# One core, two transformer-like blocks: the S5 input projection in fp32 over paired modulation rows, four rows moved, joints and head steps reordered

## The chip, the cores and the metric

The kernel runs on one core of one Trainium2 chip. The metric is the device time of one execution in microseconds. 256 tokens go through two blocks of width 2048, and all weights come from HBM in fp32, some 700 MB.

## The reference, cut to what matters

```python
def rmsnorm(x, g):
    return x * rsqrt(mean(x * x) + eps) * g
c_act = silu(c)
sh_m, sc_m, gt_m, sh_f, sc_f, gt_f = split(c_act @ w_ada + b_ada, 6)
h = rmsnorm(x, g[0]) * (1 + sc_m) + sh_m
q, k, v, g_ret, u, gate_r, gate_s = split(h @ w_in)      # u is 1024 wide
ret = head_group_norm(retention(rope(q), rope(k), v))
y_ret = (silu(g_ret) * ret) @ w_ret_out
glu_a, glu_b = split(gelu(s5_ssm(u, ...)) @ w_s5_glu)
y = (sigmoid(gate_r) * y_ret + sigmoid(gate_s) * glu_a * sigmoid(glu_b)) @ w_out
x = x + gt_m * rmsnorm(y, g[1])
h = rmsnorm(x, g[2]) * (1 + sc_f) + sh_f
x = x + gt_f * rmsnorm(swiglu(h), g[3])
# second block: attention + gated linear attention + short conv, merged,
# then a swiglu, each added to x; the end is rmsnorm(x, final gain)
```

## The kernel before

**Layout.** Everything is held transposed: features on the 128 partitions, the 256 tokens along the free axis, so `x_res` is 128 x 16 x 256. A weight tile is 128 x 2048 fp32 (1 MB): 16 k-tiles of 128 x 128 for 128 output features. The weights run through a ring of four slots. For each tile SyncE issues the load (L498) once TensorE has let the slot go (`slot_free`), ScalarE makes a rounded copy `ring_hi` (`split_hi`, L859), VectorE makes the remainder `ring_lo` (`split_lo`, L1307), and TensorE multiplies it with the activations, which are split in the same way. A product of one k-tile is three matmuls of 256 columns in the stages with `thirds` (L520, L521, L522), else one of 512 and one of 256 (L523, L524). `ahead(p, g, m)` splits tile m+2 of stage p, body g, ahead of the work on tile m.

**Modulation.** `c_act @ w_ada` isn't done on TensorE. A modulation row (1 MB: 128 output features by 2048) lies in SBUF, and VectorE multiplies it with `c_act` and sums along the free axis (`ada`, L1329), then adds the bias (`modulation`, L1334). Rows 0 to 31 (shift and scale of the first block) make up the stage "ada", where they go through the four ring slots. All later rows are "asides": they travel in the same SyncE queue between weight tiles (L507) into one of two buffers of a stage, and wait for `aside_free`, the sign that VectorE has done with that buffer's last row. Rows 32 to 35 belong to the stage "u", and rows are spread over "heads", "glu", "out1" and "down1" too.

**Stages in order**: ada; u (8 tiles, the S5 input); heads (4 bodies of 12 tiles, two retention heads each); ret (32 tiles); glu (4 bodies of 8 tiles and 4 rows); out1; ffa, ffb, down1 (the first swiglu); att, gla, conv, mrg0, mix, out2 (the second mixer); ff2, down2. In glu an even tile gives a gate (16 k-tiles), an odd one the two halves of an output (8 k-tiles each), which VectorE merges with the gate (`glu_merge`, L1616 to L1618, and `merged_lo`, L1623).

**What sets the order.** Each engine's program is written out by hand, loop body by loop body, with counting semaphores in between; SyncE's queue is in order, so a load that waits holds all behind it. Four places matter here:

- *Opening.* `x` and small tables come in beside the first rows. ScalarE squares `x` (L885), TensorE sums the squares over the partitions (`add_squares`, L569), ScalarE takes the root (L889), VectorE the reciprocal (L1354). VectorE normalises (`norm`, L1362 and L1369) when all rows are done, ScalarE applies scale and shift (L905), and the u tiles are multiplied and brought out by ScalarE (`evac`, L872).
- *Heads.* Tile m has role r = m mod 6: q, k, v, v, g, g of a head. While a head's tiles are multiplied, the head before is finished: at r = 3 VectorE takes mean and variance of `p_o` (L1531 to L1535), ScalarE the root (`ret_step(3)`, L996), VectorE reciprocal and shift (`ret_before(4)`, L1538, L1539), ScalarE the scaled copy `o_t` (`ret_step(4)`, L1000), and TensorE turns it back (`ret_back`, L635) after the product of r = 5. Beside it runs the S5 chain (L1490 to L1497 on VectorE, L1984 to L1987 on GpSimd, L587 and L597 on TensorE).
- *Joints.* After out1, down1 and down2 stands a norm of the whole residual: sum of squares (`add_squares`, `add_features`), root, reciprocal, the residual sum in 16 steps (L1390, L1394), again squares and a root, and the new h.
- *Attention.* `att_scores`, `att_turn` (L723) and `att_values` follow the products of the three tiles of a head; VectorE normalises the softmax in between (`att_before`, L1738).

```python
def split_hi(p, g, m):
    act.wait_ge(raw_in[s], p.uses(g, m) * 16)
    run(hi[s][:, 0:n, :], raw[s][:, 0:n, :], COPY)
def ahead(p, g, m):
    split_lo(p, g, m + 2)
```

## Time and profile before

| | us |
|---|---|
| median of three runs | 3454.16 |
| their spread | 3452.05 to 3454.35 |
| profiled execution, its time | 3456.49 |
| its span in the trace | 3454.6 |
| TensorE busy in it | 3298.0 (95%) |
| VectorE busy | 2389.5 (69%) |
| ScalarE busy | 1494.9 (43%) |
| GpSimd busy | 445.8 (13%) |

The profile comes from one execution. PE is TensorE, PEld its weight load, DVE VectorE, ACT ScalarE, POOL GpSimd, SP SyncE and SPq its DMA queue. "clock" is the mean of the clock granted to TensorE, as a share of full speed: 0.982 over the whole execution. The name after "L" is a line of the program above. "idle before" says how long an engine stood still ahead of an instruction and which instruction ended that.

### The profile page before, as it was taken

To read this page: it belongs to the slowest core of one execution; us is meant where nothing else is said; L and a number is where in the kernel's file an instruction comes from. 1 tells how busy PE (TensorE), PEld (TensorE's weight loads), DVE (VectorE), ACT (ScalarE), POOL (GpSimd) and SP (SyncE) were. 2 spreads that over 40 slices of the span, in tenths; PEclk is the share of its full clock that TensorE was granted. 3 is DMA by queue.
4 is the path that set the end of the run, shared out by engine and by line. 5 is a ranking of instruction groups with operands and counts; after the bars stand their busy time and mean duration, and the time that the engine had idled before them with its cause. 6 is when DMAs were issued, how large, how long until landed. Compare 5 with 4: busy or idle time off the path is not lost.

```text
span 3454.6 us, 53480 instructions
## 1 busy us (share of the span) xinstructions
PE 3298.0 (95%) x20912; PEld 2990.6 (87%) x20912; DVE 2389.5 (69%) x2467; ACT 1494.9 (43%) x1538; POOL 445.8 (13%) x309
## 2 busy tenths in 40 slices
PE   1799999999989999999989999999999999999998
PEld 0799999999978888888868888888888888888887
DVE  8799987787676666655676667657767766666554
ACT  1455555544444344433354344344344444434332
POOL 2065556720100000000000000000002100000000
PEclk7899999999999999999999999999999999999999
DMA  9665554568745555567734444555555555555554
GB/s 399 269 235 219 217 206 173 187 246 302 300 151 184 194 186 190 190 233 258 266 111 167 171 159 175 191 182 190 193 183 198 185 190 187 193 185 190 190 190 146
DMA packets 111026, 706.34 MB, mean 204 GB/s; under 512 B 13376, under 2 KB 24256, under 8 KB 30672
## 3 DMA queue, kind: packets, MB, share of 16 engines
q1 hardware_dynamic: 100416, 693.86, 54.8%
q10 hardware_dynamic: 10512, 11.11, 1.0%
q8 instruction: 69, 1.13, 0.1%
q14 instruction: 29, 0.24, 0.0%
HBM read 702.83 MB, written 2.10 MB: 204 GB/s over the span
## 4 chain that ended last, share of the span: by engine, by line
PE 82%; DVE 8%; issue 4%; ACT 3%; POOL 2%; DMA 2%; DVEq 0%; ACTq 0%; POOLq 0%; SPq 0%
PE acc L523 44%; PE acc L524 23%; PE acc L520 4%; PE acc L521 4%; PE acc L522 4%; DVE ring_lo L1307 2%; ACT ring_hi L859 1%; DMA ring_raw<-w_ada 1%; DVE ring_raw L1329 1%; POOL s_w L1985 1%; PE p_norm L569 1%; POOL s_x L1987 0%; DVE aside_y L1329 0%; PE p_y L587 0%; POOL s_x L1984 0%
## 5 line engine op out<-in xcount | busy, mean ns | idle before, releaser
L1307 DVE TENSOR_TENSOR ring_lo<-ring_raw,ring_hi 128x2048 fp32r<-128x2048 f32 (+1 forms) x576 | 1312.4, 2280 | 571.8 <-ACT ring_hi L859 570.3
L523 PE MATMUL acc<-h_split,ring_hi 128*128 128x512 f32 x4736 | 1655.5, 392 | 9.2 <-DVE h_split L1369 4.5
L524 PE MATMUL acc<-h_split,ring_lo 128*128 128x256 f32 x4736 | 1337.5, 282 | 0.0
L859 ACT ACTIVATE ring_hi<-ring_raw 128x2048 fp32r<-128x2048 f32 (+1 forms) x576 | 1070.8, 1862 | 414.4 <-DMA ring_raw<-w_down 152.0
L523 PEld LDWEIGHTS acc<-h_split,ring_hi 128*128 128x128 f32 x4736 | 891.7, 188 | 197.3 <-issue 9.7
L524 PEld LDWEIGHTS acc<-h_split,ring_lo 128*128 128x128 f32 x4736 | 897.7, 190 | 0.4
L523 PE MATMUL acc<-ffn_split,ring_hi 128*128 128x512 f32 x1408 | 488.2, 390 | 0.0
L520 PE MATMUL acc<-h_split,ring_hi 128*128 128x256 f32 x1408 | 403.7, 287 | 82.9 <-DVE h_split L1369 69.8
L1926 POOL TENSOR_TENSOR sq_sum<-sq_sum,tile 128x256 f32<-128x256 f32 x60 | 76.6, 1277 | 2568.9 <-ACT tile L885 2568.9
L524 PE MATMUL acc<-ffn_split,ring_lo 128*128 128x256 f32 x1408 | 397.1, 282 | 0.0
L521 PE MATMUL acc<-h_split,ring_hi 128*128 128x256 f32 x1408 | 396.3, 281 | 0.0
L522 PE MATMUL acc<-h_split,ring_lo 128*128 128x256 f32 x1408 | 395.8, 281 | 0.0
L520 PEld LDWEIGHTS acc<-h_split,ring_hi 128*128 128x128 f32 x1408 | 267.9, 190 | 86.9 <-issue 82.9
L523 PEld LDWEIGHTS acc<-ffn_split,ring_hi 128*128 128x128 f32 x1408 | 264.4, 188 | 55.4
L521 PEld LDWEIGHTS acc<-h_split,ring_hi 128*128 128x128 f32 x1408 | 268.0, 190 | 0.8
L522 PEld LDWEIGHTS acc<-h_split,ring_lo 128*128 128x128 f32 x1408 | 267.9, 190 | 0.0
L524 PEld LDWEIGHTS acc<-ffn_split,ring_lo 128*128 128x128 f32 x1408 | 266.1, 189 | 0.0
L1140 ACT ACTIVATE ffn_split<-ffn_a 128x256 f32 (+1 forms) x88 | 36.8, 419 | 363.8 <-DVE ffn_a L1683 363.8
L1322 DVE TENSOR_REDUCE ffn_b<-acc 128x256 f32<-128x512 f32 x88 | 60.9, 692 | 146.3 <-PE acc L524 146.3
L885 ACT ACTIVATE tile<-x_res 128x256 f32 (+1 forms) x80 | 33.1, 417 | 150.3 <-DVE x_res L1907 83.9
L1138 ACT ACTIVATE ffn_t<-ffn_a 128x256 f32<-128x256 f32 x88 | 36.8, 418 | 130.3 <-DVE ffn_a L1679 119.1
L523 PE MATMUL acc<-mixed_split,ring_hi 128*128 128x512 f32 x256 | 89.9, 393 | 0.0
(342 smaller groups left out, 3814.2 us busy)
## 6 DMA issues: line engine op xcount, KB each, us to landing
ring_raw<-w_ff SPq DMA_DIRECT2D x88, 1024.0 KB, 4.8
ring_raw<-w_down SPq DMA_DIRECT2D x64, 1024.0 KB, 4.8
ring_raw<-w_ffb SPq DMA_DIRECT2D x56, 1024.0 KB, 4.8
ring_raw<-w_heads SPq DMA_DIRECT2D x48, 1024.0 KB, 4.8
ring_raw<-w_mix SPq DMA_DIRECT2D x48, 1024.0 KB, 4.8
ring_raw<-w_ada SPq DMA_DIRECT2D x32, 1024.0 KB, 7.4
ring_raw<-w_ret SPq DMA_DIRECT2D x32, 1024.0 KB, 4.8
ring_raw<-w_glu SPq DMA_DIRECT2D x32, 1024.0 KB, 4.9
```

The costliest lines, as they stand in the source:

```text
L520: mm(dst[:, 0:T], hi[s][:, t, :], moving[:, k, 0:T], start=start, stop=False)
L521: mm(dst[:, 0:T], hi[s][:, t, :], moving[:, k, T:], start=False, stop=False)
L522: return mm(dst[:, 0:T], lo[s][:, t, :], moving[:, k, 0:T], start=False, stop=stop)
L523: mm(dst[:], hi[s][:, t, :], moving[:, k, :], start=start, stop=False, skip_group_check=True)
L524: return mm(dst[:, T:], lo[s][:, t, :], moving[:, k, 0:T], start=False, stop=stop, skip_group_check=True)
L569: mm(p_norm[:, 0:T], ones[:], tile[kt % 2][:], start=kt == 0, stop=kt == KT - 1).then_inc(sq_used, 1)
L859: run(hi[s][:, 0:n, :], raw[s][:, 0:n, :], COPY).then_inc(hi_done, 1)
L1138: run(t[i % 2][:], a[i % 2][:], ACT.Tanh, scale=0.5).then_inc(f_tanh, 1)
L1140: run(dst[:, 4 * g + (first + i), 0:T], a[i % 2][:], COPY, scale=0.5).then_inc(f_hi, 1)
L1307: tt(lo[s][:, 0:n, :], raw[s][:, 0:n, :], hi[s][:, 0:n, :], SUB).then_inc(lo_done, 1)
L1322: v.tensor_reduce(dst, acc[o % 2][:].rearrange("p (c t) -> p t c", c=2), AX_X, ADD).then_inc(sum_done, 1)
L1926: tt(sq_sum[:], sq_sum[:], tile[b][:], ALU.add).then_inc(sq_used, 1)
```

## The change

It does five things.

1. **ada and u become one stage.** The 32 rows load in pairs, shift and scale of the same features, k and k+16, into four row buffers (`aside_y`, `aside_v`, `aside_u`, `aside_c`). The eight u tiles have places of their own (`u_weights`, and the raw buffers of ring slots 2 and 3) and load between the pairs, and so do the first two tiles of heads. VectorE has 16 steps of two rows and one `mod`, and takes the norm products between them. ScalarE applies scale and shift in place and makes h. TensorE multiplies in fp32 (no hi and lo): for each k-tile eight matmuls of 128 x 256 into eight banks. The lo part of h is made on GpSimd, in 16 subtractions.
2. **Rows 32 to 35 move from u to glu**, one to a body, as a fifth row (block number 12) in `aside_u`; VectorE takes it at the end of a body. SyncE's order in glu is a list, `GLU_ORDER`. The gain of out1 (`gain[:, 1]`) is made after glu.
3. **Joints.** The residual sums run over groups of feature tiles; in out1 the gain is applied when ScalarE brings the outputs out, in the last norm it is applied by ScalarE, and VectorE multiplies by the broadcast `rstd` in groups. Squares go through four buffers instead of two.
4. **Heads.** ScalarE brings v out ahead of the root of the head before; VectorE takes mean and variance after the S5 chain's part, and reciprocal and shift behind the `split_lo` of that tile. In ret the last head's steps stand one tile earlier.
5. **Attention.** Turn one tile later, values with the next head's first tile.

```diff
+        U_LOADS = {0: (0, 1), **{k: (k + 1,) for k in range(1, HALF - 1)}}
+        HEAD_LOADS = [5, 7]
+        GLU_ORDER = [(0, b) for b in (0, 1, 3, 4, 6, 7, 9, 2, 10, 5)] + [
+            (1, 0), (0, 8), (1, 1), (0, 11), (1, 3), (0, 12), (1, 4), (1, 2), (1, 6), (1, 7), (1, 5), (1, 9), (1, 10), (1, 8), (1, 11)]
+        for later in (2, 3):
+            GLU_ORDER += [(later, 0), (later, 1), (later - 1, 12)] + [(later, b) for b in range(2, 12)]
+        GLU_ORDER += [(3, 12)]
+
+        SUM_GROUPS = [(0, 2), (2, 2), (4, 4), (8, 4), (12, 2), (14, 1), (15, 1)]
+        OUT_GROUPS = [(0, 1), (1, 1), (2, 2), (4, 4), (8, 4), (12, 2), (14, 2)]
...
+            ada, p = dram["w_ada"].rearrange("g (j p c) -> (g j) p c", j=4, p=P), ph["u"]
+            for k in range(KT):
+                for r in range(2):
+                    n, use = (2 * k + r) % 4, (2 * k + r) // 4
+                    if use:
+                        sp.wait_ge(row_free[n], use)
+                    elif n == 3:
+                        sp.wait_ge(c_made, 1)
+                    sp.dma_start(row[n][:], ada[k + KT * r]).then_inc(row_in[n], 16)
+                for o in U_LOADS.get(k, ()):
+                    src = dram["w_u"][o // 4, p.offsets[o % 4]:p.offsets[o % 4] + KT * P * P].rearrange("(p c) -> p c", p=P)
+                    sp.dma_start(u_w[o][:].rearrange("p k c -> p (k c)"), src).then_inc(u_in, 16)
+                if k in HEAD_LOADS:
+                    m = HEAD_LOADS.index(k)
+                    at = ph["heads"].offsets[m]
+                    sp.dma_start(raw[m][:].rearrange("p k c -> p (k c)"), dram["w_heads"][0, at:at + KT * P * P].rearrange(
...
                         m, i = p.weights_until(at), p.asides_until(at)
-                        src = dram["w_" + name][g, offset:offset + n * P * P].rearrange("(p c) -> p c", p=P)
+                        if at < len(p.blocks):
+                            (kind, n), offset = p.blocks[at], p.offsets[at]
+                            src = dram["w_" + name][g, offset:offset + n * P * P].rearrange("(p c) -> p c", p=P)
+                        else:
+                            (kind, n), offset = ph["u"].blocks[4 + g % 2], ph["u"].offsets[4 + g % 2]
+                            src = dram["w_u"][g // 2, offset:offset + n * P * P].rearrange("(p c) -> p c", p=P)
...
+                            if name == "heads" and opening(g) and m < SLOTS:
+                                sp.wait_ge(u_summed, 2 * m - 2)
...
+            pe.wait_ge(std_done, 1)
+            pe.wait_ge(u_in, 16 * HALF)
+            for k in range(KT):
+                pe.wait_ge(now_done, k + 1)
+                for o in range(HALF):
+                    ins = mm(u_bank[o][:, 0:T], u_w[o][:, k, :], normed[:, k, T:], start=k == 0, stop=k == KT - 1)
+                    if k == KT - 1:
+                        ins.then_inc(u_summed, 1)
+                if k < KT - 1:
+                    ins.then_inc(u_used, 1)
...
+            def first_h():
+
+                act.wait_ge(n_done, KT)
+                for k in range(KT):
+                    act.wait_ge(mod_done, k + 1)
+                    run(normed[:, k, T:], normed[:, k, T:], ACT.Identity, bias=mod[:, k:k + 1],
+                        scale=mod[:, KT + k:KT + k + 1]).then_inc(now_done, 1)
+                    act.wait_ge(now_done, k + 1)
+                    run(h[:, k, 0:T], normed[:, k, T:], COPY).then_inc(n_hi, 1)
+                    if k - 2 in HEAD_LOADS:
+                        split_hi(ph["heads"], 0, HEAD_LOADS.index(k - 2))
+                    if k == 6:
+                        waves(0, 0)
+                    elif k == 8:
+                        cosines(0, 0)
+                for o in range(HALF):
+                    act.wait_ge(u_summed, o + 1)
+                    run(u[:, o, :], u_bank[o][:, 0:T], COPY).then_inc(u_done, 1)
...
-                        if r in (3, 4):
+                        if r == 4:
                             ret_step(r, g, i, n)
                     evac(p, g, m, m, (qk[:, 0, :], qk[:, 1, :], v_t[:, 0, :], v_t[:, 1, :], g_t[:, 0, :], g_t[:, 1, :])[r])
-                    if r == 0 and not (opening(g) and i == 0):
+                    if r in (0, 3) and not (opening(g) and i == 0):
                         ret_step(r, g, i, n)
                     if r == 3:
                         if not (opening(g) and i == 0):
...
-                                square_of(stage, acc[o % 2][:, 0:T], d, o % 2)
-                                evac(p, g, o, m, y[:, d, :])
+                                square_of(stage, acc[o % 2][:, 0:T], d, o)
+                                run(y[:, d, :], acc[o % 2][:, 0:T], ACT.Identity, scale=gain[:, 1, one(d)]).then_inc(evac_done, 1)
...
+                                if updates == 3:
+                                    run(x[:, d, :], x[:, d, :], ACT.Identity, scale=gains[:, 6, one(d)]).then_inc(x_scaled, 1)
...
+            act.wait_ge(gain_done, 1)
             down(ph["out1"], 1, y1, 1)
...
+                for j, (k0, n) in enumerate(SUM_GROUPS):
+                    for k in range(k0, k0 + n):
+                        ins = stt(y[:, k, :], y[:, k, :], gain[:, i, k:k + 1], rstd[:], MUL, MUL)
+                    ins.then_inc(y_times, 1)
+                    dve.wait_ge(y_times, len(SUM_GROUPS) + j + 1)
+                    at = slice(k0, k0 + n)
+                    tt(x[:, at, :], x[:, at, :], y[:, at, :], ADD).then_inc(y_done, n)
...
+            for k in range(KT):
+                at = 2 * (k % 3)
+                if k >= 3:
+                    dve.wait_ge(mod_done, k - 2)
+                for r in range(2):
+                    n, use = (2 * k + r) % 4, (2 * k + r) // 4
+                    ada(row[n][:], row_in[n], row_free[n], use + 1, at + r)
+                for r in range(2):
+                    dve.wait_ge(row_free[(2 * k + r) % 4], (2 * k + r) // 4 + 1)
+                both = slice(k, k + KT + 1, KT)
+                stt(mod[:, both], ada_sum[:, at:at + 2], 0.5, b_ada[:, both], MUL, ADD).then_inc(mod_done, 1)
...
+                if 3 <= k < 7:
+                    for t in range(4 * k - 12, 4 * k - 8):
+                        stt(normed[:, t, T:], x[:, t, :], gains[:, 0, t:t + 1], rstd[:], MUL, MUL).then_inc(n_done, 1)
+                if k - 3 in HEAD_LOADS:
+                    split_lo(ph["heads"], 0, HEAD_LOADS.index(k - 3))
...
-                    if prev[i] and r == 4:
-                        ret_before(r, g, i, n)
                     ahead(p, g, m)
-                    if prev[i] and r != 4:
+                    if prev[i] and r != 3:
                         ret_before(r, g, i, n)
                     s5_turned_back("heads", g, m)
+                    if prev[i] and r == 3:
+                        ret_before(r, g, i, n)
...
+                i = p.asides
+                ada(aside["glu"][0][:], aside_in[0], aside_free[0], p.aside_count(g, i), i)
+                dve.wait_ge(aside_free[0], p.aside_count(g, i))
+                own.step(stt(mod[:, one(g + 2 * KT)], ada_sum[:, i:i + 1], 0.5, b_ada[:, one(g + 2 * KT)], MUL, ADD))
                 own.leave(1 if opening(g) else p.iters - 1)
+            tt(gain[:, 1, :], mod[:, 2 * KT:3 * KT], gains[:, 1, :], MUL).then_inc(gain_done, 1)
...
-            residual(y1, 1, 2)
+            inverse_std(2)
+            dve.wait_ge(evac_done, ph["out1"].out_count(ph["out1"].iters - 1, 3))
+            for j, (k, n) in enumerate(SUM_GROUPS):
+                at = slice(k, k + n)
+                tt(y1[:, at, :], y1[:, at, :], rstd[:].unsqueeze(1).to_broadcast([P, n, T]), MUL).then_inc(y_times, 1)
+                dve.wait_ge(y_times, j + 1)
+                tt(x[:, at, :], x[:, at, :], y1[:, at, :], ADD).then_inc(y_done, n)
...
-                if r == 1:
+                if r == 2:
...
-            for kt in range(KT):
-                stt(x[:, kt, :], x[:, kt, :], gains[:, 6, kt:kt + 1], rstd[:], MUL, MUL).then_inc(out_ready, 1)
+            for k, n in OUT_GROUPS:
+                dve.wait_ge(x_scaled, k + n)
+                tt(x[:, k:k + n, :], x[:, k:k + n, :], rstd[:].unsqueeze(1).to_broadcast([P, n, T]), MUL).then_inc(out_ready, 1)
...
+            for k in range(KT):
+                pool.wait_ge(n_hi, k + 1)
+                if k < KT - 1:
+                    pool.wait_ge(u_used, k + 1)
+                else:
+                    pool.wait_ge(u_summed, HALF)
+                tt(h[:, k, T:], normed[:, k, T:], h[:, k, 0:T], ALU.subtract).then_inc(h_done, 1)
```

SyncE in glu, at the seam of two bodies (here bodies 1 and 2; 2 and 3 read alike). `slot_free` counts ring slots, `aside_free0` is that of `aside_u`. Before:

```order
L507 DMA aside_u<-w_glu 128x2048 [waits aside_free0,s5_done]
L507 DMA aside_s<-w_glu 128x2048 [waits aside_free1,s5_done]
L446 UNCONDITIONAL_BRANCH
L446 ISA
L498 ISA [waits slot_free0]
L498 DMA ring_raw0<-w_glu 128x2048
L498 ISA [waits slot_free1]
L498 DMA ring_raw1<-w_glu 128x2048
L506 REGISTER_ALU [waits s5_done]
L507 ISA [waits aside_free0]
L507 DMA aside_u<-w_glu 128x2048
L498 ISA [waits slot_free2]
```

With the change:

```order
L555 DMA aside_s<-w_glu 128x2048 [waits aside_free1,s5_done]
L544 DMA ring_raw0<-w_glu 128x2048 [waits slot_free0]
L544 DMA ring_raw1<-w_glu 128x2048 [waits slot_free1]
L555 DMA aside_u<-w_u 128x2048 [waits aside_free0,s5_done]
L555 DMA aside_u<-w_glu 128x2048 [waits aside_free0,s5_done]
L544 DMA ring_raw2<-w_glu 128x2048 [waits slot_free2]
L544 DMA ring_raw3<-w_glu 128x2048 [waits slot_free3]
```

Two rows for the same buffer now stand one behind the other, with the tiles for slots 2 and 3 behind them. At the way out of glu the fifth row of body 3 stands ahead of `x_res` and of the first tiles of out1:

```order
L544 DMA ring_raw3<-w_glu 128x2048 [waits slot_free3]
L555 DMA aside_s<-w_glu 128x2048 [waits aside_free1,s5_done]
L555 DMA aside_u<-w_u 128x2048 [waits aside_free0,s5_done]
L519 DMA x_res<-x_t 128x4096 [waits s5_done]
L459 UNCONDITIONAL_BRANCH
L459 ISA
L544 ISA [waits slot_free0]
L544 DMA ring_raw0<-w_out1 128x2048
```

In order before, `x_res` followed the `aside_s` row at once.

VectorE in heads at r = 3 and 4 (`gn_` are the retention norm's values, `s5_` the S5 chain's). Before:

```order
L1307 TENSOR_TENSOR ring_lo1<-ring_raw1,ring_hi1 128x2048 [waits hi_done]
L1531 BN_STATS gn_stats<-p_o 128x6 [waits ret_summed]
L1532 BN_STATS gn_stats<-p_o 128x6
L180 REGISTER_ALU
L1533 MEMSET gn_shift 128x2 [waits dve_own]
L1534 BN_AGGR gn_mean<-gn_stats 128x2
L1535 BN_AGGR gn_mean<-gn_stats 128x2
L1483 REGISTER_ALU
L1490 TENSOR_TENSOR s5_w<-p_z,s5_tab0 128x512 [waits s5_sine,scan_done,s5_cos,z_done]
```

With the change the S5 part comes first, and behind the statistics stands the next tile's lo, then the reciprocal:

```order
L1577 SCALAR_TENSOR_TENSOR s5_w<-s5_r,s5_w 128x256
L1611 BN_STATS gn_stats<-p_o 128x6 [waits ret_summed]
L1612 BN_STATS gn_stats<-p_o 128x6
L181 REGISTER_ALU
L1613 MEMSET gn_shift 128x2 [waits dve_own]
L1614 BN_AGGR gn_mean<-gn_stats 128x2
L1615 BN_AGGR gn_mean<-gn_stats 128x2
L1392 REGISTER_ALU
L1393 TENSOR_TENSOR ring_lo2<-ring_raw2,ring_hi2 128x2048 [waits hi_done]
L1618 RECIPROCAL gn_mean<-gn_mean 128x2 [waits ret_std]
L181 REGISTER_ALU
L1619 SCALAR_TENSOR_TENSOR gn_shift<-gn_mean 128x2 [waits dve_own]
```

So the scale of a finished head now waits for `ring_lo2`, which waits for ScalarE's `ring_hi2`.

## Rows read from the trace of the kernel before

**Rows 1.** The page: busy time by engine
```profile
PE 3298.0 (95%) x20912; PEld 2990.6 (87%) x20912; DVE 2389.5 (69%) x2467; ACT 1494.9 (43%) x1538; POOL 445.8 (13%) x309
```

**Rows 2.** Timeline of the opening: start, us, engine, line, operation [idle before]
```profile
37.49 0.16 DVE L1334 SCALAR_TENSOR_TENSOR mod<-ada_sum,b_ada_sb 128x4 f32 x1 [0.25 <-DVE ada_sum L1329]
...
98.05 1.91 ACT L859 ACTIVATE ring_hi<-ring_raw 128x2048 fp32r<-128x2048 f32 x1 [59.01 <-DMA ring_raw<-w_u]
...
106.99 0.55 PE L520 MATMUL acc<-h_split,ring_hi 128*128 128x256 f32 x1 [69.81 <-DVE h_split L1369]
...
155.69 1.28 ACT L937 ACT_TABLE_LOAD   x1
```

**Rows 3.** Busy time by stretch: length, PE, PEld, DVE, ACT, POOL; clock; DMA share; GB/s
```profile
20.00:40.00 20.00, 11.00 (x32) 5.95 (x32) 18.52 (x36) 10.29 (x22) 14.02 (x12) 1.00 1.00 403
...
401.00:405.00 4.00, 4.00 (x20) 4.00 (x20) 1.93 (x2) 3.31 (x6) 0.00 (x0) 0.50 0.00 0
```

**Rows 4.** Timeline of TensorE: heads, second head of a body; end of glu
```profile
399.35 0.58 PE L520 MATMUL acc<-h_split,ring_hi 128*128 128x256 f32 x1 [3.24 <-ACT v_t L872]
...
892.95 0.39 PE L520 MATMUL acc<-merged_split,ring_hi 128*128 128x256 f32 x1 [1.23 <-DVE merged_split L1623]
```

**Rows 5.** Timelines of ScalarE and TensorE in heads, first head of a body
```profile
353.69 0.29 ACT L996 ACTIVATE gn_mean<-gn_mean,eps 128x2 f32<-128x2 f32 x1 [9.03 <-DVE gn_mean L1535]
...
356.28 1.90 ACT L859 ACTIVATE ring_hi<-ring_raw 128x2048 fp32r<-128x2048 f32 x1
...
361.64 0.60 PE L635 MATMUL p_norm<-ident,o_t 128*128 128x128 f32 x4
```

**Rows 6.** Groups by line in the joint after out1: busy, mean ns | idle before
```profile
L1390 DVE SCALAR_TENSOR_TENSOR y<-y,gain,rstd 128x256 f32 x16 | 6.7, 480 | 0.4 <-DVE rstd L1354 0.4
L1394 DVE TENSOR_TENSOR x_res<-x_res,y x16 | 5.7, 419 | 0.0
```

**Rows 7.** Timeline and groups of TensorE in attention
```profile
1803.64 0.33 PE L723 MATMUL p_z<-ident,ex 128*128 128x128 f32 x1 [3.33 <-DVE ex L1738]
...
L723 PE MATMUL p_z<-ident,ex 128*128 128x128 f32 x4 | 1.1, 285 | 2.2 <-DVE ex L1738 2.2
```

**Rows 8.** Timeline of TensorE: fp32 matmuls of 256 columns, two records each
```profile
184.87 1.02 PE L587 MATMUL p_y<-s_x,s_c_sb 128*128 128x256 f32 x4
185.74 1.03 PE L597 MATMUL p_z<-u,s_b_sb 128*128 128x256 f32 x4
```

**Rows 9.** Timelines of GpSimd and VectorE side by side, in heads
```profile
360.67 3.39 DVE L1329 CUSTOM_DVE_ANT_0 aside_r<-aside_r,c_act 128x2048 f32<-128x2048 f32 x1
...
361.99 2.67 POOL L1986 TENSOR_TENSOR s_x<-s_w,s_x 128x256 f32<-128x256 f32 x1
...
363.99 2.81 DVE L1307 TENSOR_TENSOR ring_lo<-ring_raw,ring_hi 128x2048 fp32r<-128x2048 f32 x1
```

**Rows 10.** Timeline of VectorE in glu: end of body 1, and in body 3
```profile
801.86 0.43 DVE L1623 SCALAR_TENSOR_TENSOR merged_split<-val_a,merged_split 128x256 f32 x1 [0.72 <-ACT merged_split L1075]
...
874.25 2.28 DVE L1329 CUSTOM_DVE_ANT_0 aside_u<-aside_u,c_act 128x2048 f32<-128x2048 f32 x1
```

**Rows 11.** Timeline of SyncE's queue at a seam of glu and at its end
```profile
792.57 5.77 SPq L498 DMA_DIRECT2D ring_raw<-w_glu  x2
...
866.20 0.34 SPq L481 DMA_DIRECT2D x_res<-x_t  x1
869.94 5.77 SPq L498 DMA_DIRECT2D ring_raw<-w_out  x2
```

**Rows 12.** The page: loads, KB each, us from issue to landing
```profile
ring_raw<-w_ff SPq DMA_DIRECT2D x88, 1024.0 KB, 4.8
```

**Rows 13.** Timeline of ScalarE in glu and at the start of out1
```profile
806.22 0.38 ACT L872 ACTIVATE val_a<-acc 128x256 f32<-128x256 f32 x1 [0.53 <-PE acc L522]
...
880.79 1.92 ACT L859 ACTIVATE ring_hi<-ring_raw 128x2048 fp32r<-128x2048 f32 x1 [5.15 <-DMA ring_raw<-w_out]
...
899.34 0.39 ACT L885 ACTIVATE tile<-acc 128x256 f32<-128x256 f32 x1 [1.38 <-PE acc L522]
```

More of the change, by code:

```diff
@@ L95, in asides_in @@
     def asides_in(self, k):
-        return len(range(k, self.asides, self.beside))
+        return len(range(k, self.rows, self.beside))
     def aside_count(self, g, i):
@@ L131, in schedule @@
     }
-    for name in ("u", "ffa", "att"):
+    for name in ("ffa", "att"):
         ph[name].opens = True
-        ph[name].opening_lo = 4 if name == "u" else 3
-    for name in ("u", "heads", "ret", "glu", "out1"):
+        ph[name].opening_lo = 3
+    for name in ("heads", "ret", "glu", "out1"):
         ph[name].thirds = True
+    ph["glu"].rows += 1
     block = weight = 0
@@ L1454, in _ @@
[L1454 to L1466 removed]
+            own.step(v.tensor_scalar(b_ada[:, KT:2 * KT], b_ada[:, KT:2 * KT], 1.0, None, ADD))
@@ L1625, in _ @@
             for g in bodies(dve, p, first=1):
-                own.enter(4 * 2 + 1 + opening(g), g, first=1)
+                own.enter(4 * 2 + 2 + opening(g), g, first=1)
                 if opening(g):
```

228 lines of the change are left out of this document (110 added, 118 removed).

## The prediction

> **What bounds the kernel now.** I began with the page. TensorE is busy 3298.0 us of a span of 3454.6 [rows 1]. So an edit counts where it moves TensorE's work or an idle time of TensorE; a VectorE step beside a running product is free. I then read the timelines of the changed stages for the places where TensorE stands still.
>
> In the opening it sums squares and then waits 69.81 us, until 106.99 [rows 2]. DMA fills that time: its share is 1.00, at 403 GB/s [rows 3]. The hi of the first u tile starts at 98.05, when the tile has landed; 36.4 MiB have come by then (c 1, tables 0.4, x 2, 32 rows, one tile) since about 1.8 us, so 2.64 us per MiB. The last u output comes out just ahead of 155.69 [rows 2]: heads begins at 155.2. In glu TensorE idles only at the end, 1.23 us [rows 4]: nothing is to be gained there, but much to lose. In heads it waits once per body, 3.24 us, for ScalarE's copy of v [rows 4], which stands behind a root that waits for VectorE as in [rows 5]. After that wait the granted clock is 0.50, the lower of its two levels, 1.2 of 2.4 GHz [rows 3]; the product behind it took 8.5 us, where others take 5.6. I charge that difference, 2.9 us, to every idle time of three us or more. In a joint VectorE's 32 steps are the path, TensorE idle [rows 6]; in attention it waits for the softmax [rows 7].
>
> **The change, part by part** (minus is a gain).
>
> *Opening.* Three clocks run side by side. **DMA**: the last row is now the 45.4th MiB (32 rows, 8 u tiles, 2 heads tiles, 3.4 else) and lands at 1.8 + 45.4 x 2.64 = 121.8. **TensorE**: two fp32 matmuls take 0.87 us [rows 8], so the 128 take 55.7. They can start when row 13 (the 25.4th MiB, 69.0) is multiplied and the last norm products are made, at 74.2, and would end at 74.2 + 55.7 + 2.9 = 132.8. **VectorE**: a pair costs two rows at 2.25 and 0.6 for `mod` (0.16, with 0.25 of waiting before it and as much behind) [rows 2], 5.1 in all. Pair 8 is done at 87.6, since its rows land no sooner; seven more pairs and two lo parts of 2.3 give 127.9. On top come GpSimd's subtractions, some twelve in that stretch. In heads a row took 3.39 us beside GpSimd, 1.1 more than the usual 2.29, and a lo part 2.81, 0.5 more than usual [rows 9]. At 0.8 each that is 9.6: the last `mod` at 137.5, 0.5 on ScalarE and 3.5 for the last eight matmuls, 141.5. Heads begins **13.7** earlier. Ends: -22.4 if GpSimd costs nothing and TensorE's own work binds, -6 if all sixteen cost 1.1. Heads tiles 2 and 3 load only after `u_summed` 2 and 4, but land some 7 us later and are needed 11 us later: free.
>
> The Trainium skill, SBUF — State Buffer, section "Who interferes with whom", says that a VectorE operation with two SBUF inputs and a GpSimd one that reads SBUF exclude each other, and the one that comes second is blocked for the other's whole length. By that rule each of the twelve would cost its full length, and the opening would give 10.1, the sum below 3483. The rows bear out that they exclude each other, but one of the two lost only 0.5 us.
>
> *Rows 32 to 35.* Their VectorE work, 4 x 2.3 us, lies beside products wherever it stands. What counts is SyncE's queue. In glu's bodies 2 and 3, row (g-1, 12) is followed by the first row of body g for the same buffer, which waits until VectorE has taken the former, at the end of body g-1: `merged_lo` at 801.86 [rows 10], then the row until 804.6. Behind it wait the tiles for slots 2 and 3, issued at 792.57 before [rows 11], now at 805.3. A tile lands 4.8 after its issue [rows 12], 2.6 more behind another MiB: 812.8. ScalarE makes that tile's hi ahead of bringing out the gate, and TensorE needs the gate's bank for the second half product, which began at about 806.3, where `val_a` comes out [rows 13]. Now it begins at 812.8 + 1.9 + 0.4 = 815.1: idle 8.8, clock 2.9, **+11.5** rounded, twice. In body 1 the row stands loosely among its tiles: free.
>
> At the way out, row (3, 12) waits for that buffer's last row, done at 876.5 [rows 10], and `x_res` and out1's tiles stand behind it; before, they went at 866.20 and 869.94 [rows 11], and the hi of the first began at 880.79 [rows 13]. Now x, a row and a tile (4 MiB) follow 876.5: the hi starts at 888.8, the gate's bank is 7.9 late, and the clock costs 2.9. Then out1's first row waits for row (3, 12), multiplied behind the end of glu: 892.9 [rows 4], plus 8 to 8.5, plus 2.3, is 903.6. Out1's tile 2 stands behind: it lands at 911.3 and its lo is ready at 915.5, 918.4 with the clock's loss. Its product began at 898.9, just as the one before came out [rows 13]. That is **+19.6** for the whole way out. Glu in all: **+42.6**, low end 28 (no clock loss), high end 50.
>
> *Heads.* In the second head of a body the wait for v goes, -3.24 - 2.9, and `ret_back` then waits 1.3. But a head's scale now stands behind the next tile's lo, hence behind a hi, which ScalarE makes after the root and two exponentials. In the first head of bodies 1 to 3 the variance comes behind the S5 part, 3.9 us later than the root's 353.69; so the hi of 356.28 [rows 5] starts at 359.9, its lo ends past 364, and the shift is ready at 365.4. TensorE turned `o_t` back at 361.64 [rows 5] and would want it at 360.5: idle 4.9, clock 2.9, less 0.9 of an S5 wait that goes. Net 2.7 a body and **+8** in all, ends -18 (nothing is late) and +14 (a fall of the clock in every second head too).
>
> *Joints.* After out1, 16 steps of 0.480 become broadcast ones at the 0.419 of a plain sum [rows 6], -1.0; and the first group has two tiles instead of four (2 x 0.48) and the last one instead of four, -1.6. After down1 the latter alone. **-2.6 - 1.6**, ends 0 and -3.6 each (a whole group's 4 x 0.90). *Attention.* The 3.33 and the 2.2 [rows 7] go, with 1.6 of slow clock: **-7**, ends -10 and -3 (another step waits instead). *End.* As at the first joint, **-1**. *Ret*: no idle time there, 0, ends +-3.
>
> Sum: -13.7 + 42.6 + 8 - 2.6 - 1.6 - 7 - 1 = **+24.7**. The profiled execution took 3456.5 and would take 3481.2; the median of the runs is 2.3 lower, so the forecast is **3479 us**.
>
> **Rivals.** Less than 0.2% (6.9 us) can't be told from no change.
>
> *A, faster: the queue doesn't hold the tiles back.* If the slot-2 tile's hi is made by 804 at both seams and out1's first by 881, the 42.6 go: **3436**. The wait on `aside_free0` would have to be met by a row earlier than I read it, or VectorE to take the fifth row by 793, ahead of `merged_lo`. For it: VectorE idles in glu. Against: the written order. Half of the price gives 3458.
>
> *B: heads works as meant.* Nothing is late behind the lo, -18 instead of +8: **3453**. It decides whether that hi can start before some 355; against it, the variance stands behind the S5 part.
>
> *C: GpSimd costs VectorE nothing* in the opening, -22.4: **3470**. For it: where the row comes first, it is GpSimd that waits, as its 2.67 us for a quarter of the elements show [rows 9].
>
> *D: every subtraction costs its full length*, 12 x 1.1 = 13.2 instead of 9.6, as blocked operations would: **3483**. It is what the Trainium skill's page above would have.
>
> **How the numbers follow.** Forecast 0.38 (alone 3464 to 3490), C 0.11, D 0.11, B 0.15, A 0.25 with its half. Faster: A in full and B where the opening is cheap too, 0.17 + 0.06 = 0.23. Same (3447.3 to 3461.0): B else and half A, 0.09 + 0.08 = 0.17. Slower 0.60. The range leaves out about a tenth at either side: 3436 to 3488.
>
> **What would show it.** Right: in glu SyncE issues the second `aside_u` row of a seam right after a VectorE row at a body's end; the hi behind it waits some 8 us for DMA; TensorE idles 8 to 9 us at two seams and twice around out1's start, clock 0.5 behind each. The first heads product begins near 141. In the first head of a body `ret_back` waits for `o_t`; no product waits for v. Wrong: no idle time over 3 us in glu (A), no wait for `o_t` (B), the first heads product at 133 (C) or 145 (D).

## The result and the profile after

The changed kernel takes 3487.43 us (three runs, 3486.97 to 3487.54) where the kernel before takes 3454.16: a ratio of 1.0092, 95% interval 1.0077 to 1.0108, so 33 us slower. The profiled execution has a span of 3485.1, 30.5 more than that of before, at a mean clock of 0.979. The page, busy time by engine:

```profile
PE 3320.6 (95%) x20784; PEld 3012.0 (86%) x20784; DVE 2358.5 (68%) x2417; ACT 1494.2 (43%) x1562; POOL 468.0 (13%) x325
```

TensorE executes 128 matmul records fewer than in [rows 1] and is still busy 22.6 us more; its mean granted clock is 0.979 where it was 0.982. To see where the 30.5 us come from, I read the same event in both traces, stage by stage; the difference of two lines is the stage's own cost. These are single executions, and the opening's pace differs by 1 to 2 us from run to run, as the runs below show.

| event | before | after | after - before | stage's own | forecast |
|---|---|---|---|---|---|
| first q of heads comes out | 161.88 | 141.58 | -20.3 | opening -20.3 | -13.7 |
| last g of heads comes out | 496.37 | 484.75 | -11.6 | heads +8.7 | +8 |
| fourth gate of glu comes out | 729.95 | 728.92 | -1.0 | ret +10.6 | 0 |
| last output of out1 comes out | 978.49 | 1014.52 | +36.0 | glu and out1 +37.1 | +42.6 |
| first norm product after joint 1 | 999.12 | 1033.03 | +33.9 | joint 1 -2.1 | -2.6 |
| first norm product after joint 2 | 1759.38 | 1792.96 | +33.6 | joint 2 -0.3 | -1.6 |
| first output of out2 | 2623.1 | 2653.6 | +30.5 | attention -3.1 | -7 |
| end of the span | 3454.6 | 3485.1 | +30.5 | the end 0 | -1 |

**Glu.** The timeline of SyncE's queue at the first seam and at the way out, which answers to [rows 11]:

```profile
786.79 0.33 SPq L555 DMA_DIRECT2D aside_u<-w_u  x1
803.18 0.33 SPq L555 DMA_DIRECT2D aside_u<-w_glu  x1
803.56 0.90 SPq L544 DMA_DIRECT2D ring_raw<-w_glu  x2
...
886.12 0.33 SPq L555 DMA_DIRECT2D aside_s<-w_glu  x1
897.17 0.33 SPq L555 DMA_DIRECT2D aside_u<-w_u  x1
897.55 0.42 SPq L519 DMA_DIRECT2D x_res<-x_t  x1
898.31 1.01 SPq L544 DMA_DIRECT2D ring_raw<-w_out  x2
923.82 0.33 SPq L555 DMA_DIRECT2D aside_u<-w_out  x1
924.34 0.85 SPq L544 DMA_DIRECT2D ring_raw<-w_out  x2
```

The queue stands from 786.79 to 803.18, though the ring slot of the next tile was free by about 792 (that tile goes at 792.57 in [rows 11]): it waits for this VectorE row, the fifth of body 1, which comes behind `merged_lo` (timeline of VectorE):

```profile
800.47 0.43 DVE L1703 SCALAR_TENSOR_TENSOR merged_split<-val_a,merged_split 128x256 f32 x1 [0.72 <-ACT merged_split L1153]
800.81 2.28 DVE L1415 CUSTOM_DVE_ANT_0 aside_u<-aside_u,c_act 128x2048 f32<-128x2048 f32 x1
```

The tiles that are issued behind it are waited for by ScalarE, and the gate comes out behind the hi (timeline of ScalarE):

```profile
810.56 1.91 ACT L928 ACTIVATE ring_hi<-ring_raw 128x2048 fp32r<-128x2048 f32 x1 [10.27 <-DMA ring_raw<-w_glu]
812.38 0.36 ACT L941 ACTIVATE gate<-acc 128x256 f32<-128x256 f32 x1
```

and TensorE has four long idle times where before there were none, two at seams, one at the way out and one in out1 (timeline of TensorE):

```profile
812.79 0.58 PE L568 MATMUL acc<-y_ssm_split,ring_hi 128*128 128x256 f32 x1 [8.01 <-ACT gate L941]
...
868.47 0.58 PE L568 MATMUL acc<-y_ssm_split,ring_hi 128*128 128x256 f32 x1 [7.95 <-ACT gate L941]
...
911.88 0.58 PE L568 MATMUL acc<-y_ssm_split,ring_hi 128*128 128x256 f32 x1 [7.77 <-ACT gate L941]
...
935.36 0.58 PE L568 MATMUL acc<-merged_split,ring_hi 128*128 128x256 f32 x1 [6.68 <-DVE ring_lo L1393]
```

They add up to 30.4 us. The first matmul after each takes 0.58 us where one at full clock takes 0.28, as after the wait of 3.24 in [rows 4], and the granted clock from 814 to 818, from 913 to 917 and from 936 to 940 is 0.50: the clock has fallen again. The stage also no longer has the 1.23 us of [rows 4], so 37.1 + 1.2 - 30.4 = 7.9 us are left for the four falls, 2.0 each. TensorE's busy time between the same two events says so too: 254.97 us against 247.09 before, for the same products.

**Opening.** VectorE's rows, GpSimd's subtractions and ScalarE's first outputs of u (timelines):

```profile
90.28 2.81 DVE L1415 CUSTOM_DVE_ANT_0 aside_u<-aside_u,c_act 128x2048 f32<-128x2048 f32 x1
93.02 2.80 DVE L1415 CUSTOM_DVE_ANT_0 aside_c<-aside_c,c_act 128x2048 f32<-128x2048 f32 x1
...
95.93 0.49 DVE L1536 SCALAR_TENSOR_TENSOR mod<-ada_sum,b_ada_sb 128x2 f32<-128x2 f32 x1
...
131.37 0.16 DVE L1536 SCALAR_TENSOR_TENSOR mod<-ada_sum,b_ada_sb 128x2 f32<-128x2 f32 x1
...
88.10 35.99 POOL L2107 TENSOR_TENSOR h_split<-normed,h_split 128x256 fp32r<-128x256 f32 x13
...
132.96 0.81 ACT L1015 ACTIVATE u<-acc 128x256 f32<-128x256 f32 x2 [0.34 <-PE acc L659]
```

TensorE's fp32 stretch starts at 74.03, as forecast (74.2). The last `mod` is made at 131.37, not at 121.8 with the last load nor at 137.5. Each of the thirteen subtractions in the merged POOL line takes 2.77 us, mostly waiting, and from 90.28 on eight rows take 2.80 instead of 2.28 and six `mod` 0.49 instead of 0.16: about one VectorE operation is held up per subtraction. The first output of u comes out at 132.96 and heads starts at 136, 19 us earlier than before.

**Heads and ret.** By the groups of the whole trace TensorE waits for the scaled copy `o_t`, and at the start of ret once for `scores`:

```profile
L688 PE MATMUL p_norm<-ident,o_t 128*128 128x128 f32 x32 | 7.1, 360 | 22.8 <-ACT o_t L1083 22.8
L680 PE MATMUL p_o<-v_n,scores 128*128 128x256 f32 x16 | 5.3, 418 | 3.7 <-DVE scores L1627 3.7
```

Before, these idle times were 2.0 and none, and 11.0 stood at v, which has gone. In the first head of bodies 1 to 3 the wait for `o_t` is 4.4 to 4.5 us, forecast 4.9; here one of them, and the longest, in ret (timeline of TensorE):

```profile
348.44 1.11 PE L688 MATMUL p_norm<-ident,o_t 128*128 128x128 f32 x4 [4.43 <-ACT o_t L1083]
...
513.85 1.12 PE L688 MATMUL p_norm<-ident,o_t 128*128 128x128 f32 x4 [5.70 <-ACT o_t L1083]
```

In ret the last head's scale waits longest. ScalarE's timeline there:

```profile
504.13 0.29 ACT L1079 ACTIVATE gn_mean<-gn_mean,eps 128x2 f32<-128x2 f32 x1
504.44 1.28 ACT L1020 ACT_TABLE_LOAD   x1
505.74 0.63 ACT L1020 ACTIVATE s_sin<-s_ph 128x512 f32<-128x512 f32 x1
...
507.55 1.89 ACT L928 ACTIVATE ring_hi<-ring_raw 128x2048 fp32r<-128x2048 f32 x1
512.78 1.02 ACT L1083 ACTIVATE o_t<-p_o,gn_shift,gn_mean 128x256 f32<-128x256 f32 x2 [3.34 <-DVE gn_shift L1619]
```

The variance was there at 501.8. The root waits for an output and a table, then come a second table, two sines with an absolute value between them, and only then the hi on whose lo the scale now waits.

**Joints and attention.** Groups of four feature tiles as one broadcast product, against [rows 6], and the softmax wait against [rows 7]:

```profile
1020.89 1.22 DVE L1748 TENSOR_TENSOR y<-y,rstd 128x1024 f32<-128x1024 f32 x1
1022.21 1.23 DVE L1750 TENSOR_TENSOR x_res<-x_res,y 128x1024 f32<-128x1024 f32 x1
...
L780 PE MATMUL p_z<-ident,ex 128*128 128x128 f32 x8 | 2.3, 285 | 2.9 <-DVE ex L1829 2.9
```

### The profile page after: what moved, and what is told of

Read it like the earlier page. It is cut to its first block, busy times and chain, and to the rows that moved or that the text cites. A ratio compares the mean times of both kernels' runs of the same rounds, so it can differ in the third digit from the quotient of the medians.

```text
span 3485.1 us, 52775 instructions
## 1 busy us (share of the span) xinstructions
PE 3320.6 (95%) x20784; PEld 3012.0 (86%) x20784; DVE 2358.5 (68%) x2417; ACT 1494.2 (43%) x1562; POOL 468.0 (13%) x325
## 4 chain that ended last, share of the span: by engine, by line
PE 80%; DVE 10%; ACT 3%; issue 3%; DMA 2%; POOL 1%; ACTq 0%; DVEq 0%; SPq 0%; POOLq 0%
PE acc L571 43%; PE acc L572 23%; PE acc L568 4%; PE acc L569 4%; PE acc L570 4%; DVE ring_lo L1393 3%; ACT ring_hi L928 1%; DMA aside_v<-w_ada 1%; DVE aside_u L1415 1%; DVE aside_y L1415 1%; DMA s_d_sb<-s_d 1%; PE p_norm L617 1%; DVE aside_v L1415 1%; DMA ring_raw<-w_out 1%; PE p_z L645 0%
## 5 line engine op out<-in xcount | busy, mean ns | idle before, releaser
L1393 DVE TENSOR_TENSOR ring_lo<-ring_raw,ring_hi 128x2048 fp32r<-128x2048 f32 (+2 forms) x568 | 1292.5, 2277 | 626.6 <-ACT ring_hi L928 625.4
L572 PE MATMUL acc<-h_split,ring_lo 128*128 128x256 f32 x4736 | 1337.5, 282 | 0.0
L928 ACT ACTIVATE ring_hi<-ring_raw 128x2048 fp32r<-128x2048 f32 (+2 forms) x568 | 1054.8, 1861 | 380.5 <-DMA ring_raw<-w_down 146.8
L571 PEld LDWEIGHTS acc<-h_split,ring_hi 128*128 128x128 f32 x4736 | 891.6, 188 | 197.5 <-issue 9.7
L572 PEld LDWEIGHTS acc<-h_split,ring_lo 128*128 128x128 f32 x4736 | 897.7, 190 | 0.4
L568 PE MATMUL acc<-h_split,ring_hi 128*128 128x256 f32 x1280 | 369.2, 288 | 0.3 <-ACT val_a L941 0.2
L569 PE MATMUL acc<-h_split,ring_hi 128*128 128x256 f32 x1280 | 361.0, 282 | 0.0
L570 PE MATMUL acc<-h_split,ring_lo 128*128 128x256 f32 x1280 | 360.8, 282 | 0.0
L568 PEld LDWEIGHTS acc<-h_split,ring_hi 128*128 128x128 f32 x1280 | 245.1, 192 | 2.7 <-DVE ring_lo L1393 1.1
L569 PEld LDWEIGHTS acc<-h_split,ring_hi 128*128 128x128 f32 x1280 | 244.8, 191 | 1.0
L570 PEld LDWEIGHTS acc<-h_split,ring_lo 128*128 128x128 f32 x1280 | 244.3, 191 | 0.0
L568 PE MATMUL acc<-y_ssm_split,ring_hi 128*128 128x256 f32 x256 | 74.9, 293 | 23.8 <-ACT gate L941 23.7
```

Of the source, the lines that this page charges most:

```text
L568: mm(dst[:, 0:T], hi[s][:, t, :], moving[:, k, 0:T], start=start, stop=False)
L569: mm(dst[:, 0:T], hi[s][:, t, :], moving[:, k, T:], start=False, stop=False)
L570: return mm(dst[:, 0:T], lo[s][:, t, :], moving[:, k, 0:T], start=False, stop=stop)
L571: mm(dst[:], hi[s][:, t, :], moving[:, k, :], start=start, stop=False, skip_group_check=True)
L572: return mm(dst[:, T:], lo[s][:, t, :], moving[:, k, 0:T], start=False, stop=stop, skip_group_check=True)
L928: run(hi[s][:, 0:n, :], raw[s][:, 0:n, :], COPY).then_inc(hi_done, 1)
```

## The experiments

The theory after the comparison: the loss is a queue that holds tiles behind a waiting row (37 us), and two orders of steps (19 us); the opening gains 20. The rivals: the rows' own work on VectorE is what glu pays, and heads and ret lose because the new opening hands them over late.

Kernels differ from the changed one by the edits shown. Ratios are to the kernel before on the same chip, where it took 3455.8 to 3457.7 us.

**The queue in glu.** At the seams, and (for the run on both) at the way out, tiles go ahead of the row that waits:

```diff
-            GLU_ORDER += [(later, 0), (later, 1), (later - 1, 12)] + [(later, b) for b in range(2, 12)]
-        GLU_ORDER += [(3, 12)]
+            GLU_ORDER += [(later, 0), (later, 1), (later - 1, 12), (later, 3), (later, 4), (later, 2)] + [(later, b) for b in range(5, 12)]
+        # not shown: out1, first body: blocks 0, 1, then row (3, 12), then 3, 4, 2, 5
```

> The changed kernel, but in SyncE's queue the tiles of slots 2 and 3 stand ahead of the row that waits for VectorE, at both seams of glu, and x_res and the first tiles of out1 stand ahead of the last row. The same rows are loaded and multiplied. Theory (the queue holds the tiles back): the idle times of TensorE for the gate and for out1's third tile go, the stretch from glu's start to out1's end gives back about 35 of its 37 us, 3452 us. Rival (the four rows' work on VectorE is what glu pays): the time stays within 5 us of 3487.

Measured: 3449.77 us, 0.9973 (0.9962 to 0.9985): 41 us less than the changed kernel by the ratios, 1.0092 - 0.9973, 38 by the medians and 35.8 by the spans. The rival falls. The queue now reads (timeline of SyncE's queue):

```profile
787.92 0.33 SPq L560 DMA_DIRECT2D aside_u<-w_u  x1
792.17 5.77 SPq L549 DMA_DIRECT2D ring_raw<-w_glu  x2
804.32 0.33 SPq L560 DMA_DIRECT2D aside_u<-w_glu  x1
```

The tiles go at 792.17, as in [rows 11], and the row waits behind them until 804.32. Of TensorE's idle times between 780 and 930 us only this is left (groups of TensorE):

```profile
L573 PE MATMUL acc<-merged_split,ring_hi 128*128 128x256 f32 x115 | 32.4, 282 | 2.3 <-DVE merged_split L1708 1.2 <-DVE ring_lo L1398 1.1
```

The same rows are loaded and multiplied, so their work isn't what glu pays. This edit alone turns the change from a loss of 0.9% into a gain of 0.3%.

> The changed kernel with the tiles of slots 2 and 3 ahead of the waiting row at the two seams of glu alone; the way out of glu as changed. Theory (each seam costs its 8.0 us of idle time and 2.9 of slow clock): 22 us less, 3465, and 15 us are left for the way out. Rival (the way out carries more, since delays at the seams are made good by it): 8 to 15 us less.

Measured: 3468.29 us, 1.0035 (1.0022 to 1.0048), 20 us less by the ratios, 18.2 by the spans (3466.9). The two seams cost about 9 to 10 us each, less than the 11 of the theory, and the way out the other half.

**Heads and ret.** One edit puts ret back, another VectorE's order in heads, another ScalarE's:

```diff
 # ret: the last head's steps one tile later again (TensorE's part; ScalarE's and VectorE's not shown)
-                    if opening(g) and m in (0, 2):
-                        steps[3 * m // 2 + 2](ph["heads"].iters, 0, HEADS)
+                    if opening(g) and m in (1, 3):
+                        steps[3 * m // 2 + 1](ph["heads"].iters, 0, HEADS)
 # heads, VectorE
+                    if prev[i] and r == 4:
+                        ret_before(r, g, i, n)
                     ahead(p, g, m)
-                    if prev[i] and r != 3:
+                    if prev[i] and r != 4:
                         ret_before(r, g, i, n)
                     s5_turned_back("heads", g, m)
-                    if prev[i] and r == 3:
-                        ret_before(r, g, i, n)
 # heads, ScalarE
-                        if r == 4:
+                        if r in (3, 4):
                             ret_step(r, g, i, n)
                     evac(...)
-                    if r in (0, 3) and not (opening(g) and i == 0):
+                    if r == 0 and not (opening(g) and i == 0):
```

With ret alone put back:

> The changed kernel with the steps of the last head in ret back in the order of before; heads as changed. Theory (these steps, one tile earlier, cost 10.6 of the 18 us): 3477, and the 5.7 us wait for o_t and the 3.7 us wait for scores there are gone or small. Rival (the waits there are handed down from heads, which hands over late): within 3 us of 3487.

Measured: 3479.04 us, 1.0067 (1.0050 to 1.0084). By the spans 8.4 us less (3476.7), and the fourth gate comes out 10.4 us earlier than before the change instead of 1.0: ret costs nothing again, heads still its 8.8. Less than the 10 forecast: 1 us of it is the start of heads, which this run had 1 us later. So the two orders lose separately.

With all three put back:

> The changed kernel with the heads and ret steps back in the order of before, all else as changed. Theory (the new order delays o_t by a hi and a lo, and in ret by two tables besides): the 22.8 us for o_t and the 3.7 for scores go, the 11 for v come back, heads and ret cost what they did: 18 us less, 3469. Rival (the stages lose because the new opening hands them over in another state, with tiles 2 and 3 late): the time stays near 3487.

Measured: 3469.72 us, 1.0034 (1.0022 to 1.0047), 20 us less by the ratios, 17.8 by the spans. Heads and ret pass this run's head start of 19.9 us on whole (20.0 at the fourth gate). The loss is the order's; the new opening has no part in it.

With ret and VectorE's order put back, and v still brought out first:

> As the run before, but in heads ScalarE still brings v out ahead of the root of the head before; VectorE and ret are in the order of before. Theory (v first is the good half of the edit): the three waits of 3.24 us and the slow clock behind each go and nothing else is late: 18 less than the run before, 3451. Rival (the root moved behind v is late for the scale, so o_t waits instead): within 4 us of the run before, 3469.

Measured: 3468.59 us, 1.0032 (1.0021 to 1.0044), the same as the run before. The forecast of 18 us fell, but the rival wasn't right either: it isn't `o_t` that waits instead. Groups of TensorE in the run before, with v behind the root:

```profile
L568 PE MATMUL acc<-h_split,ring_hi 128*128 128x256 f32 x1280 | 366.0, 286 | 11.5 <-ACT v_t L941 10.0 <-DVE ring_lo L1391 1.3 <-ACT val_a L941 0.2
```

The same groups in this one:

```profile
L568 PE MATMUL acc<-h_split,ring_hi 128*128 128x256 f32 x1280 | 364.3, 285 | 11.2 <-DVE ring_lo L1391 11.0 <-ACT val_a L941 0.2
```

The 10.0 us for v, in three long waits, have become 11.0 us for lo parts, in ten waits of 2.0 at most. In the second head of a body VectorE is what is late (timeline of VectorE in this run):

```profile
367.93 1.78 DVE L1633 TENSOR_TENSOR qk_rot<-qk,rope_sb 128x512 f32<-128x512 f32 x1
369.73 2.83 DVE L1635 TENSOR_TENSOR qk_sin<-qk,rope_sb 64x512 f32<-64x512 f32 x2
372.59 1.12 DVE L1637 TENSOR_TENSOR qk_rot<-qk_rot,qk_sin 128x512 f32<-128x512 f32 x1
373.63 3.37 DVE L1391 TENSOR_TENSOR ring_lo<-ring_raw,ring_hi 128x2048 fp32r<-128x2048 f32 x1
376.93 0.42 DVE L1609 BATCH_NORM_STATS2 gn_stats<-p_o 128x6 f32<-128x256 f32 x1
```

Rotation and the lo part come one behind the other, and the statistics behind both. Before, TensorE met that lateness as one wait for v; now it meets it in smaller pieces at the lo parts. The busy times from 250 to 450 us in this run (length, PE, PEld, DVE, ACT, POOL; clock, DMA, GB/s) say the same:

```profile
250.00:450.00 200.00, 190.60 (x1516) 184.61 (x1516) 182.45 (x190) 114.02 (x140) 110.40 (x67) 1.00 0.60 222
```

The clock no longer falls (1.00, where the kernel before has 0.97 in that stretch and the run with v behind the root 0.99), and yet hardly more matmuls are done: 1516 records, against 1500 and 1513. So there was a new theory: heads is bound by VectorE. Four kernels test it, below.

**GpSimd beside VectorE.** `pool.wait_ge(u_used, k + 1)` becomes `pool.wait_ge(u_summed, HALF)` for all k.

> The changed kernel, but GpSimd makes the lo parts of h only after the last fp32 matmul, so that nothing runs beside VectorE's rows. Theory (each subtraction costs VectorE about 0.52 us): the last mod is ready near 127 instead of 131.5, and the last of the fp32 matmuls ends near 133, TensorE's own pace, instead of 135.7; heads then waits 16 to 18 us for GpSimd, so the whole is 12 to 16 us slower, about 3501. Rival (the loads set VectorE's pace): the last mod stays at 131.

Measured: 3499.86 us in one execution, 12.4 more than the changed kernel, as the theory had it. The last `mod`, and GpSimd's sixteen subtractions by themselves (timelines):

```profile
126.73 0.16 DVE L1536 SCALAR_TENSOR_TENSOR mod<-ada_sum,b_ada_sb 128x2 f32<-128x2 f32 x1
...
132.47 15.04 POOL L2104 TENSOR_TENSOR h_split<-normed,h_split 128x256 fp32r<-128x256 f32 x16 [43.81 <-PE p_norm L659]
```

From 90 us on every row takes 2.28 or 2.29 us and every `mod` 0.16, the last `mod` is 4.6 us earlier, and a subtraction by itself takes 0.94 us. The opening's pace isn't the same in every run: VectorE's first lo part of heads begins at 88.08 in the changed kernel, at 88.61 in this one, and between 87.57 and 90.05 in the others. Counted from there, GpSimd delays the last `mod` of the changed kernel by 5.2 us.

**Together.** "The first run" is that on the queue, "the third" that with v brought out first.

> The queue edit of the first run and the head order of the third together; the opening, the joints and the attention steps as changed. Theory (the losses lie in different stages and add up): 41 and 21 us less than the changed kernel in the same measure, 0.991 of before, 3424 to 3430 us, faster than both kernels. Rival (one loss hid the other): less than 10 us under the first run.

Measured: 3430.92 us, 0.9928 (0.9911 to 0.9944). The theory's 0.991 lies at the edge of the interval; by the spans the gains, 35.8 and 18.5, add up to 54.3 of the 56.4 measured (3485.1 to 3428.7). The losses are separate.

The subtractions on VectorE, behind its last row, and taken out of GpSimd's program (not shown). The kernel that this one starts from, and is compared with, is the run just shown:

```diff
             dve.wait_ge(mod_done, KT)
+            for k in range(KT):
+                dve.wait_ge(n_hi, k + 1)
+                if k < KT - 1:
+                    dve.wait_ge(u_used, k + 1)
+                else:
+                    dve.wait_ge(u_summed, HALF)
+                tt(h[:, k, T:], normed[:, k, T:], h[:, k, 0:T], SUB).then_inc(h_done, 1)
```

> As the first kernel of this call, and the 16 lo parts of h are made by VectorE behind its last mod, not by GpSimd beside the rows. Theory (a subtraction beside a row costs VectorE 0.52, and behind the rows it has nothing else to do): the last mod near 127 instead of 131.5, TensorE's fp32 stretch ends near 131, the last lo part near 134, and heads starts 2 us earlier than in the first kernel of this call. Rival (16 x 0.42 us at the end are as long as what they save): the same within 1 us.

Measured: 3427.07 us, 0.9916 (0.9899 to 0.9933), 3.9 us under the run before it on the same chip (3.3 by the spans). The timeline of VectorE:

```profile
128.58 5.45 DVE L1556 TENSOR_TENSOR h_split<-normed,h_split 128x256 fp32r<-128x256 f32 x16
```

All sixteen take 5.45 us there, 0.34 each, and the first q comes out at 139.68 instead of 142.6. Counted from the first lo part (90.05 and 89.08) the opening is 3.9 us shorter, twice what the theory said.

**Is heads bound by VectorE?** Two by two, on this last kernel: v first or behind the root, and the modulation rows multiplied in full or a quarter of their columns in heads (`[:, 0:(512 if name == "heads" else D)]`). The short rows leave out three quarters of each sum, so those two kernels don't compute the reference; they only price VectorE's work.

> e8_sub_on_vector, but in heads VectorE multiplies only 512 of the 2048 columns of each modulation row (the load, the waits and all else stay; the modulation values come from a part of the row). Theory (with v brought out first, heads is bound by VectorE at the second head, so the edit gained 1 us where 18 were there): the 11 us of waits for ring_lo and the slow clock behind each go, 15 to 20 us less, near 3410. Rival (the lo parts wait for ScalarE or for DMA): within 4 us of 3427.

> As e11_short_rows, but ScalarE brings v out behind the root, as before the change. Theory (the root waits for VectorE's statistics, which come sooner with less to do, so here too most of the wait goes): between e11_short_rows and 6 us above it. Rival (the wait for v is set by something else than VectorE's load): 18 us above e11_short_rows.

> e8_sub_on_vector with v brought out behind the root. Theory (VectorE's load sets the time either way): 1 us slower than e8_sub_on_vector, 3428. Rival (with the queue mended, v first is worth its full wait): 10 to 18 us slower.

| | rows in full | rows short |
|---|---|---|
| v first | 3427.07 (0.9916) | 3408.64 (0.9863) |
| v behind the root | 3426.44 (0.9914) | 3410.22 (0.9867) |

The intervals of the two short ones are 0.9847 to 0.9880 and 0.9851 to 0.9883, that of 0.9914 is 0.9898 to 0.9931. Less VectorE work gives 18 us with v first and 16 with v behind; the order of v gives 1.6 us at most. All three theories hold, and none of the rivals. Groups of TensorE with short rows and v first:

```profile
L573 PE MATMUL acc<-h_split,ring_hi 128*128 128x256 f32 x1280 | 365.0, 285 | 1.8 <-DVE ring_lo L1396 1.3 <-ACT val_a L946 0.4
```

The 11 us are gone, and no other idle time took their place. The busy time of the engines from 250 to 450 us, in the kernel before:

```profile
250.00:450.00 200.00, 191.38 (x1500) 187.01 (x1500) 183.68 (x192) 113.88 (x139) 112.63 (x68) 0.97 0.58 218
```

And with short rows and v first:

```profile
250.00:450.00 200.00, 199.11 (x1598) 195.11 (x1597) 169.84 (x201) 116.24 (x144) 113.61 (x71) 1.00 0.62 236
```

With VectorE at 91 to 92% of the stretch TensorE waits in both orders of v; at 85% it waits for next to nothing, 0.9 us in 200, at full clock. The share alone doesn't tell it: in the changed kernel, whose order makes VectorE wait for ScalarE, VectorE is busy 84% of that stretch and TensorE still idles 14.8 us. And part of VectorE's time there goes with GpSimd, which runs beside it: a lo part takes 2.50 us on average, where one by itself takes 2.28 (compare [rows 9]). No run takes GpSimd's S5 work out of heads, so its share in the bound stays open.

**Attention.** The turn one tile earlier again and the values with the head's own third tile.

> The fastest kernel so far (e8_sub_on_vector, 3427) with the attention steps back in the order of before. Theory (the new order took away 2.6 us of TensorE's waits for the softmax and some slow clock): 3 us slower, 3430. Rival (the 3 us by which the stretch from the second swiglu to the merge got shorter come from the joint): the same as e8_sub_on_vector.

Measured: 3429.68 us, 0.9921 (0.9904 to 0.9937) against 0.9916. The two intervals can't tell 3 us from nothing; the trace can, in one execution of each: from the first output of the first swiglu to the first of out2 it is 2.7 us longer (988.4 to 2596.1 against 989.0 to 2594.0), and TensorE's wait is the one of before again:

```profile
L785 PE MATMUL p_z<-ident,ex 128*128 128x128 f32 x8 | 2.3, 285 | 5.5 <-DVE ex L1821 5.5
```

The fastest versions that compute the reference are two, with v first or behind: the changed one's opening, joints and attention, the old order of ret and of VectorE in heads, the tiles ahead of the waiting rows in glu, and the subtractions on VectorE, 0.8 to 0.9% faster than before.

## Why the prediction was right, and where it was not

It said 3479 (3436 to 3488), slower with 0.60; measured were 3487.4. The direction, the mechanism that carries it and its places were right. That the time lies inside the range, near its upper end, is in part luck: the sum was too high by 6.6 us in the opening and 5.5 in glu, too low by 10.6 in ret, 3.9 in attention and 3.5 in the rest, and most of that cancels. Ret and attention alone would have put it at 3493, outside.

*Rows 32 to 35, +42.6.* Right in every link: the second `aside_u` row was to be issued at 804.6 and was at 803.18; the idle times at the seams and at the way out were to be 8.8, 8.8 and 7.9 and were 8.01, 7.95 and 7.77; the fourth, in out1, has no length of its own in the prediction and was 6.68. The stage measured +37.1, 5.5 less than the term; mis-sized were the clock's loss behind each, put at 2.9, where 2.0 remains (3.6 in all), and the idle times at the seams (1.6). Rival A falls, since the wait on `aside_free0` is met only at a body's end; the run on the queue shows that the queue alone costs 35.8 of span.

*Opening, -13.7.* Measured -19 to -20. VectorE sets its end, as said, but the term for GpSimd was too high: 0.8 a subtraction was taken, 0.52 was lost on a row (2.80 against 2.28) and 0.33 on a `mod`, and the run with late subtractions puts the sum at 5.2 us, not 9.6. Without them VectorE was to be done at 127.9, and in that run it was at 126.73. Rivals C (nothing) and D (1.1 each) are both out. (C's 2.67 us is for an eighth of a row's elements, not for a quarter.) The Trainium skill's rule that the second comer is blocked for the other's whole length (SBUF — State Buffer, "Who interferes with whom") holds here in kind: GpSimd's operations stretch from 0.94 to 2.77 us beside the rows, 1.8 more. For VectorE the rows show about half of that length, 0.52 of 0.94, as price.

*Heads, +8.* Measured +8.7 and caused as written: variance behind the S5 part, scale behind a lo behind a hi. But the ends of that term (-18 if nothing is late), and with it rival B, rested on a false step: that the wait of 3.24 us and the clock behind it are there to be had once v is brought out first. With VectorE's and ret's order put back it gave 1 us, not clear of the noise, because VectorE's lateness shows up at the next lo parts. The profile of before had the sign of it: VectorE 92% busy in that stretch, which I didn't read as a bound.

*Ret, 0.* Wrong: +10.6. The step that failed is "no idle time there, 0": nothing waited in ret before, so moving its steps one tile earlier was taken to cost nothing. I looked for an idle time that could go, not for what the moved steps would find ahead of them: two table loads and two sines on ScalarE, then a hi and its lo. It is the same delay as in heads, met at a place with still more in ScalarE's queue, and the largest miss of the sum.

*Joints, -2.6 and -1.6.* -2.1 and -0.3. In the second only the sum is grouped, and each group waits for its products (0.1 us, once 0.5), which takes back what a shorter first and last group give. *Attention, -7.* -3.1: the wait went from 5.5 to 2.9, not to 0. *The end, -1.* 0.

## What to carry to other kernels

In a queue that is served in order, put no load whose buffer comes free late ahead of loads whose buffers are free already: here a few entries of an order table, with no work added to any engine, decided between 0.9% slower and 0.3% faster. Before steps are moved ahead of an idle time, read what stands in the queues of all engines they pass through at the new place; a step that is one tile earlier for one engine can be later for the next. And before an idle time of TensorE is counted as a gain, look how busy the engine that feeds it is in that stretch: here VectorE was busy 91 to 92% of it, a new order only moved the idle time, and less work on VectorE took it away.
